# Twelve weight slots at twelve distances from the activations, and one matrix of ones instead of two

## The reference, cut to what matters

```python
for i in range(DEPTH):                       # DEPTH = 4
    h = mixer(x)                             # x @ w_in, convolution or token mix, @ w_out
    x = layer_norm(ALPHA * x + h, ln1_g[i], ln1_b[i])
    h = (silu(x @ ffn_w_gate[i]) * (x @ ffn_w_up[i])) @ ffn_w_down[i]
    x = layer_norm(ALPHA * x + h, ln2_g[i], ln2_b[i])
    gate = sigmoid(x @ ple_w_gate[i])
    x = x + gate * rms_norm(p[i] @ ple_w_proj[i], ple_norm_g[i])
```

## Time and profile before

| | |
|---|---|
| median of 2 runs | 2546.16 us (2546.01 to 2546.31) |
| profiled execution | 2546.59 us |
| its span, first to last instruction | 2544.8 us |
| TensorE: matmul busy, weight loads busy | 2520.1 us (99%), 2314.1 us (91%) |
| DVE, ACT busy | 1955.3 us (77%), 1200.0 us (47%) |
| granted TensorE clock, mean | 0.999 |

### The profile page before, as it was taken

One profiled execution on the slowest core, in us unless ns is written; L12 is line 12 of the kernel. 1 busy time (PEld: TensorE's weight loads), 2 busy tenths in 40 slices (PEclk: granted clock), 3 DMA queues, 4 the chain that ended last, 5 costly groups with the idle time before them and its releaser, 6 DMA issues. The chain is left out here.

```text
span 2544.8 us, 41246 instructions
## 1 busy us (share of the span) xinstructions
PE 2520.1 (99%) x17241; PEld 2314.1 (91%) x17241; DVE 1955.3 (77%) x2571; ACT 1200.0 (47%) x1960; POOL 1.4 (0%) x10
## 2 busy tenths in 40 slices
PE   9999999999999999999999999999999999999999
PEld 7899999889888899998898899998898999999888
DVE  6988999577454679995784479996677979999576
ACT  6775444436233254443362245444356766444335
POOL 0000000000000000000000000000000000000000
PEclk9999999999999999999999999999999999999999
DMA  5202333324322223333233224333222203333322
GB/s 156 73 12 92 113 103 108 103 88 128 95 92 91 84 89 103 107 101 108 82 101 97 94 67 123 103 108 107 92 91 93 66 26 97 103 107 102 108 82 76
DMA packets 267054, 240.10 MB, mean 94 GB/s; under 512 B 14908, under 2 KB 212852, under 8 KB 266740
## 3 DMA queue, kind: packets, MB, share of 16 engines
q1 hardware_dynamic: 266292, 236.94, 30.2%
q10 hardware_dynamic: 576, 0.52, 0.1%
HBM read 233.21 MB, written 2.10 MB: 92 GB/s over the span
## 5 line engine op out<-in xcount | busy, mean ns | idle before, releaser
L1786 DVE TENSOR_TENSOR w_lo<-raw,w_hi 128x1024 fp32r<-128x1024 f32 x287 | 345.4, 1222 | 266.0 <-ACT w_hi L1309 265.7
L1309 ACT CAST w_hi<-raw 128x1024 fp32r<-128x1024 f32 x287 | 294.8, 1045 | 372.8 <-DMA raw<-in_ffn_w_down_dram 104.1
L879 PE MATMUL psum<-h_hi,w_lo 128*128 128x512 f32 x872 | 341.4, 392 | 0.0
L881 PE MATMUL psum<-h_hi,w_hi 128*128 128x512 f32 x872 | 339.4, 389 | 0.0
L880 PE MATMUL psum<-h_lo,w_hi 128*128 128x512 f32 x856 | 333.2, 389 | 0.0
L1024 PE MATMUL psum<-a_hi,w_lo 128*128 128x256 f32 x1088 | 280.9, 286 | 6.6 <-DVE w_lo L1786 5.1
L1024 PE MATMUL psum<-a_hi,w_hi 128*128 128x256 f32 x1088 | 277.5, 284 | 0.0
L1190 PE MATMUL psum<-h_hi,w_hi 128*128 128x256 f32 x768 | 217.3, 283 | 0.0
L1191 PE MATMUL psum<-h_hi,w_hi 128*128 128x256 f32 x768 | 217.3, 283 | 0.0
L1024 PEld LDWEIGHTS psum<-a_hi,w_lo 128*128 128x128 f32 x1088 | 209.1, 192 | 8.7 <-DVE w_lo L1786 4.6
L1024 PEld LDWEIGHTS psum<-a_hi,w_hi 128*128 128x128 f32 x1088 | 209.3, 192 | 0.3
(11 more groups left out here) (362 smaller groups left out, 6494.3 us busy)
## 6 DMA issues: line engine op xcount, KB each, us to landing
raw<-in_ffn_w_gate_dram SPq DMA_DIRECT2D x176, 256.0 KB, 3.0
raw<-in_ffn_w_up_dram SPq DMA_DIRECT2D x176, 256.0 KB, 3.3
raw<-in_ffn_w_down_dram SPq DMA_DIRECT2D x176, 256.0 KB, 3.1
raw<-in_a_w_pw_dram SPq DMA_DIRECT2D x94, 256.0 KB, 3.1
raw<-in_ple_w_gate_dram SPq DMA_DIRECT2D x64, 256.0 KB, 3.2
raw<-in_b_w_in_dram SPq DMA_DIRECT2D x64, 256.0 KB, 3.0
raw<-in_c_w_in_dram SPq DMA_DIRECT2D x48, 256.0 KB, 2.9
raw<-in_b_w_out_dram SPq DMA_DIRECT2D x32, 256.0 KB, 3.1
```

The lines of the kernel that those rows point to most:

```text
L879: pe.matmul(bank(grp.g, j), st_lo, mv_hi, start=(k == 0), stop=False, skip_group_check=by_tiles(grp))
L881: done = pe.matmul(bank(grp.g, j), st_hi, mv_hi, start=False, stop=(ku == last and a == UK - 1), skip_group_check=by_tiles(grp))
L1309: act.copy(hi_u[u % RING], raw_u[u % RING]).then_inc(hi_ready, 1)
L1786: dve.tensor_tensor(lo_u[u % RING], raw_u[u % RING], hi_u[u % RING].bitcast(F32), ALU.subtract)\
```

## The change

Each slot of `raw`/`w_lo` is shifted by its own number of words, and each slot of `w_hi` by another; the two buffers grow by 48 and 80 words to hold the shifts. `ones_r` becomes another name for the memory of `ones`, which gives back the 512 bytes that the shifts take. The float32 matmuls with ones and the two activations read `ones_r` through a float32 view.

```diff
+RAW_SHIFT = (0, 8, 16, 24, 40, 48)
+HI_SHIFT = (20, 28, 36, 44, 60, 68)
...
-        raw, raw_at = sb("raw", RING * UK * BANK)
-        w_lo = also("w_lo", RING * UK * BANK, F32R, raw_at)
-        w_hi, hi_at = sb("w_hi", RING * UK * BANK, F32R)
-        w_hi_f32 = also("w_hi_f32", RING * UK * BANK, F32, hi_at)
+        raw, raw_at = sb("raw", RING * UK * BANK + 48)
+        w_lo = also("w_lo", RING * UK * BANK + 48, F32R, raw_at)
+        w_hi, hi_at = sb("w_hi", RING * UK * BANK + 80, F32R)
+        w_hi_f32 = also("w_hi_f32", RING * UK * BANK + 80, F32, hi_at)
...
-        ones, _ = sb("ones", P)
-        ones_r, _ = sb("ones_r", P, F32R)
+        ones, ones_at = sb("ones", P)
+        ones_r = also("ones_r", P, F32R, ones_at)
...
+        ones_f = ones_r[:, :].bitcast(F32)
...
-        raw_u = [raw[:, r * UK * BANK:(r + 1) * UK * BANK] for r in range(RING)]
-        hi_f32 = [w_hi_f32[:, r * UK * BANK:(r + 1) * UK * BANK] for r in range(RING)]
-        hi_u = [w_hi[:, r * UK * BANK:(r + 1) * UK * BANK] for r in range(RING)]
-        lo_u = [w_lo[:, r * UK * BANK:(r + 1) * UK * BANK] for r in range(RING)]
+        def slots(t, shift):
+
+            return [t[:, r * UK * BANK + at:(r + 1) * UK * BANK + at] for r, at in enumerate(shift)]
+
+        raw_u, lo_u = slots(raw, RAW_SHIFT), slots(w_lo, RAW_SHIFT)
+        hi_f32, hi_u = slots(w_hi_f32, HI_SHIFT), slots(w_hi, HI_SHIFT)
...
-                pe.matmul(hcol(half_bank(s, h, 0), h), ones[:, :], hcol(tiles(tmp, 5), h), start=True, stop=True)\
+                pe.matmul(hcol(half_bank(s, h, 0), h), ones_f, hcol(tiles(tmp, 5), h), start=True, stop=True)\
```

More of the change, by code:

```diff
@@ L925, in conv_stats @@
                 pe.wait_ge(conv_sums, 4 * (s.layer // 3) + 2 * h + 1)
-                pe.matmul(hcol(half_bank(s, h, 0), h), ones[:, :], hcol(tiles(tmp, 5), h), start=True, stop=True)\
+                pe.matmul(hcol(half_bank(s, h, 0), h), ones_f, hcol(tiles(tmp, 5), h), start=True, stop=True)\
                     .then_inc(half_stats, 1)
                 pe.wait_ge(conv_sums, 4 * (s.layer // 3) + 2 * h + 2)
-                pe.matmul(hcol(half_bank(s, h, 1), h), ones[:, :], hcol(tiles(tmp, 4), h), start=True, stop=True)\
+                pe.matmul(hcol(half_bank(s, h, 1), h), ones_f, hcol(tiles(tmp, 4), h), start=True, stop=True)\
                     .then_inc(half_stats, 1)
@@ L1004, in stats_half @@
                     pe.wait_ge(z_pair, 4 * s.norm + 4)
-                last = pe.matmul(sum_z, ones[:, :], hcol(tiles(tmp, 5), h), start=True, stop=(h == 0))
+                last = pe.matmul(sum_z, ones_f, hcol(tiles(tmp, 5), h), start=True, stop=(h == 0))
                 if h == 1:
@@ L1008, in stats_half @@
                     for j in range(2):
-                        last = pe.matmul(sum_z, ones[:, :], hcol(tiles(pair_sums, j), h), start=False, stop=(j == 1))
+                        last = pe.matmul(sum_z, ones_f, hcol(tiles(pair_sums, j), h), start=False, stop=(j == 1))
                 last.then_inc(half_stats, 1)
                 pe.wait_ge(half_sums, 3 * s.norm + h + 2)
-                pe.matmul(sum_sq, ones[:, :], hcol(tiles(tmp, 4), h), start=True, stop=True).then_inc(half_stats, 1)
+                pe.matmul(sum_sq, ones_f, hcol(tiles(tmp, 4), h), start=True, stop=True).then_inc(half_stats, 1)
             def rms_sum(s):
                 pe.wait_ge(rms_sums, s.layer + 1)
-                pe.matmul(bank(s.groups[-1].g + 1, 2), ones[:, :], tiles(a_f32, PROJ_SQ), start=True, stop=True)\
+                pe.matmul(bank(s.groups[-1].g + 1, 2), ones_f, tiles(a_f32, PROJ_SQ), start=True, stop=True)\
                     .then_inc(rms_done, 1)
@@ L1220, in mix_rows @@
                 for i in range(2):
-                    last = pe.matmul(bank(s.table_g, 2 + i), ones[:, :], tiles(h_f32, W_T + i), start=True, stop=True)
+                    last = pe.matmul(bank(s.table_g, 2 + i), ones_f, tiles(h_f32, W_T + i), start=True, stop=True)
                 last.then_inc(rowsum_done, 1)
@@ L1350, in load_silu @@
                 own.settle()
-                own.add(act.activation(small[:, 121:122], ones[:, 0:1], ACT.Silu))
+                own.add(act.activation(small[:, 121:122], ones_f[:, 0:1], ACT.Silu))
             def load_sqrt():
                 own.settle()
-                own.add(act.activation(small[:, 120:121], ones[:, 0:1], ACT.Sqrt))
+                own.add(act.activation(small[:, 120:121], ones_f[:, 0:1], ACT.Sqrt))
             def no_block(t, at):
```

## The result

The changed kernel takes 2561.24 us (2 runs, 2561.24 to 2561.25) against 2546.16: ratio 1.0064, 95% interval 1.0048 to 1.0081. It is 15.1 us slower. The forecast was 2511, with 2478 to 2556 as its range: wrong in sign and outside the range. Rival B, the wide matmuls losing, had 2563; whether its reason holds is what the first experiments ask. In this kernel all lines behind the edit stand six higher: 879 is 885, 1024 is 1030, 1189 to 1191 are 1195 to 1197.

What follows compares the result with a forecast made beforehand. TensorE's own stream, the distance between matmul starts, was taken as the bound. Line 1024 -12.7, pairs -13.2 and wide matmuls -9.6 gave -35.5 us from 2546.2, rounded to 2511 us; range 2478 to 2556.

Steps and rivals of the forecast that it cites:

- Rival B: Wide matmuls never settle as distances change: 4,800 x +5 = +24 us, narrow -7, 2563 us; chance 0.15.
- What bounds the kernel: Whole kernel: TensorE's own stream is the time; what remains is how far apart two matmuls start.
- 512 columns: Wide matmuls, lines 879 to 881, 897 to 899, 869, 870, 875: -2 ns on each of 4,800, -9.6 us.
- surplus of 13.3 ns: Start-to-start time above one column a cycle, both widths; 15,072 matmuls carry it, 200 us an address edit could touch.
- the earlier trace: Profile rows before the change: last-tap durations 277 to 283 ns; six wide starts after the first wait, 232 ns each.
- 256 columns: Narrow matmuls at -3 ns: line 1024 -12.7 us, pairs (lines 1189 to 1191) -13.2 us.
- the last taps: Lines 946 to 948, the sample with varying distances: 119.2 ns between starts, 0.8 under the locked 120.
- third unit: Pairs: every third unit has unshifted high parts, only 8 of its 42 matmuls affected; share affected 0.73.
- The cover in the pair stages: DVE busy 174.4 of 181 us; a 3.3 us fall leaves some 3 us slack, at most some 4 us gain.
- DVE, ACT, loads and ones at nothing: Shifted addresses cost DVE, ACT and loads nothing, nor does sharing ones: 0, within 1 us either way.
- Rival A: Nothing happens: the 13.3 ns are a fixed cost of changing the weights; 2546 us, chance 0.15.
- Rival C: All reach the short form: line 1024 -25 us, pairs -16, wide -14 to -29; 2476 to 2491 us, chance 0.2.

Runs made afterwards that it cites:

- the first experiments: Changed kernel with all twelve slots back at distance 0, shared ones kept: 2546.56 us; all at 64 bytes: 2560.08 us; all at 128: 2565.87 us.
- the ones alone: Changed kernel with all twelve slots back at distance 0, only the shared matrix of ones kept: 2546.56 us beside 2546.5 before.

## Why the prediction was wrong

**What bounds the kernel**: right, in the pair stages too, where the kernel at distance 0 keeps its 181.3 us with less work for DVE. The distance between starts is the time, and distance 0 against another changes it with nothing else moved.

**512 columns: the step that failed.** "I take -2: 4,800 x -2 = -9.6 us." It measured +4.7 ns and +22.4 us, 32 us of the 50 by which the forecast missed. The argument was that the same surplus of 13.3 ns at both widths should react alike, and that the shortest durations of the settled stream bound the gain. It does not react alike: at distance 0 the stream has settled at 227 and 120 ns, which is the least a wide step takes at any distance tried and nearly the most a narrow one takes. The only rows of wide matmuls off that state were the earlier trace rows, 232 ns, and I gave them little weight. They came within 1 ns of the result, but they lie at distance 0 just after a wait, and no run shows that the two have one cause.

**256 columns: mis-sized.** For line 1024, -3 ns was taken and -1.6 measured, -5.8 us for -12.7. The mean of the last taps, 119.2, was closer than the best single durations of the earlier trace rows. Their durations at 144 to 208 bytes do not carry over: counted as in the prediction, 176 is the weights at 80 bytes, and its slot number had 118.7 ns. A single matmul in a stream of changing distances tells little of a uniform stream. The pairs' steps were mis-sized too: their mean fell by 1.4 ns, some 8 of the 13.2 us. (Of a third unit's 42 matmuls 6 read the slot and not 8, three products with two tiles each; the share is 0.71 and the term -13.0.)

**The cover in the pair stages: too generous.** "A stage that falls by 3.3 us ... still has some 3 us of slack." The stages fell by 1.0 us (181.3 to 180.3), and with any shift they stopped between 180.2 and 180.9. The idle time that was counted as slack was not free: with all slots at 192 it is 122 gaps between DVE's instructions, nearly all short, 6.6 us beside 173.7 us busy, together the 180.5 us of the stage. Leaving some of DVE's work out showed that DVE holds the stage; why the gaps cannot be used is only argued, from instructions that depend on each other. Of the pairs' 8 us of shorter steps waits took some 4 back: of 13.2 us 4.0 came.

**DVE, ACT, loads and ones at nothing**: right. DVE's unit operation is at 1,221 ns before and 1,220 after, and the ones alone made no difference. Of the missing 50 us, 32 are the wide term, 7 the narrow, 9 the pairs, and 2 waits between the stages.

**Rival A** (a fixed cost of changing weights) is refuted by every run that changes the distance. **Rival B** had the place and the price, +24 us wide and -7 narrow, against +22.4 and -9.8. Its reason, that a changing distance never lets the stream settle, does not hold: all slots at 64 or 128 bytes are as slow, and at 64 the stream settles at 233.3 ns. So its number came right without its mechanism. **Rival C** needed narrow steps of 114 and cover in the pairs; the first exists nearly (115.3 with all at 64, 113.3 in its settled stretches), the second does not, and no distance made the wide ones shorter.

The rule of the Trainium skill that I weighed ("TensorE: Matmul & The Clock Gate", "Step-by-step: what each phase is for": loading weights takes no read bandwidth from the running matmul) would have kept the time, as I read it. The runs disagree with that reading: with all slots at one distance the same wide matmuls have steps of 226.9 (0), 229.3 (192), 232.7 (128) or 233.0 ns (64). Whether it is read bandwidth that the load takes, no run shows.

## What to carry to other kernels

Where TensorE is bound by back-to-back matmuls, measure the distance from start to start by width, and try an address change on one uniform distance before spreading buffers over many: wide and narrow matmuls may want opposite distances. A sample taken at the state that you will leave says nothing of the state that you will enter; of the rows that show another state, take their mean and not their best. And before counting a gain of TensorE in a stage where another engine is busy above nine tenths, take that engine's whole chain, with its waits, as the floor.

## What the runs showed of the hardware that was not expected

- With weights and activations at the same remainder modulo 256 bytes the stream locks to constant steps of 120.0 and 226.7 ns, 13.3 ns above columns / 2.4 GHz in both. Moving both by 64 bytes keeps it.
- The sign of the distance counts. In the stage of layer 1 where the slot moves and the activation is stationary, all slots at 64 give 229.0 ns and all at 192 give 233.3; with the slot stationary it is the other way round, 233.3 and 229.0. So what counts is moving minus stationary: 64 gives 229.0 in both roles, 192 gives 233.3.
- At 64 bytes the stream settles too, but only in some stages (about half of line 1030, at 113.3 ns, and three in ten of the wide matmuls with stationary weights, at 233.3); elsewhere it goes round in cycles of a few values (114, 117, 118 and 119 ns). With all slots at 128 and the weights stationary no stretch of 24 constant steps exists at either width. At the granted 2.4 GHz the four settled steps are 272 and 288 cycles for 256 columns and 544 and 560 for 512.
- A step depends on its neighbours' distances too: the matmul at distance 0 between matmuls at 192 lasted 399 ns instead of 389.
- Why 0 suits the wide matmuls and 64 and 192 the narrow ones, and whether the moving read or the weight load is held up, stays open.
